# Expert weights loaded as 768 pieces of half a megabyte instead of 384 of one, on a decoder layer with 32 experts

## The reference

```
x = x + W_out( sigmoid(Ga h) * HGRN2(h) + sigmoid(Gb h) * MultiScalePool(h) ),   h = RMSNorm(x)
x = x + MoE_top4of32(RMSNorm(x))
x = x + sigmoid(RMSNorm(x) W_pg) * (p W_pp),   then a final RMSNorm

gate = min(xb @ w_gate[e] + b_gate[e], 7);  up = clip(xb @ w_up[e] + b_up[e], -7, 7)
y    = ((up + 1) * gate * sigmoid(1.702 * gate)) @ w_down[e] + b_down[e]
```

## Time and profile before

| | |
|---|---|
| median of 3 runs | 1330.59 us |
| the profiled execution's own time | 1328.84 us |
| its span | 1326.8 us |
| TensorE busy | 1236.3 us, 93% of the span |
| VectorE, ScalarE, GpSimd busy | 25%, 14%, 5% |
| moved by DMA | 462.48 MB, 349 GB/s over the span |
| mean granted TensorE clock | 0.99 |

### The profile page before, as it was taken

One profiled execution on the slowest core, in us unless ns is written; L12 is line 12 of the kernel. 1 busy time (PEld: TensorE's weight loads), 2 busy tenths in 40 slices (PEclk: granted clock), 3 DMA queues, 4 the chain that ended last, 5 costly groups with the idle time before them and its releaser, 6 DMA issues.

```text
span 1326.8 us, 15719 instructions
## 1 busy us (share of the span) xinstructions
PE 1236.3 (93%) x6207; PEld 563.6 (42%) x6207; DVE 331.1 (25%) x644; ACT 179.1 (14%) x353; POOL 72.5 (5%) x155
## 2 busy tenths in 40 slices
PE   6999998999999999999998989899899989999996
PEld 5755444465443443434333333434333333434332
DVE  2423435043412212122111212112111212212123
ACT  3315213112100101101000101101000101100022
POOL 7021120030000000000000000000000000000001
PEclk9999998998999999999999999999999999999999
DMA  9836372394499999999999999999999999999950
GB/s 331 276 126 237 116 285 65 129 386 175 168 422 420 422 422 422 422 422 422 422 422 422 422 422 422 422 422 421 423 422 422 422 421 423 422 422 420 422 227 34
DMA packets 80531, 462.48 MB, mean 349 GB/s; under 512 B 8681, under 2 KB 9865, under 8 KB 31344
## 3 DMA queue, kind: packets, MB, share of 16 engines
q1 hardware_dynamic: 73968, 444.16, 81.7%
q0 software_dynamic: 3840, 12.85, 3.1%
q10 hardware_dynamic: 2688, 4.98, 1.1%
HBM read 456.04 MB, written 6.39 MB: 349 GB/s over the span
## 4 chain that ended last, share of the span: by engine, by line
PE 70%; DMA 24%; DVE 2%; ACT 1%; issue 1%; SPq 1%; POOLq 0%; POOL 0%; DVEq 0%; ACTq 0%
PE bank L1016 34%; DMA arena<-in_w_down_dram 22%; PE bank L660 10%; PE bank L1073 5%; PE bank L702 3%; PE bank L957 3%; PE bank L1107 2%; PE bank L852 2%; DMA arena<-in_w_up_dram 2%; PE bank L683 1%; PE bank L967 1%; PE bank L1037 1%; PE bank L629 1%; SPq L426 1%; PE bank L984 1%
## 5 line engine op out<-in xcount | busy, mean ns | idle before, releaser
L1016 PE MATMUL bank<-arena 128*64 128x512 f32 x3072 | 678.6, 595 | 46.5 <-DMA arena<-in_w_up_dram 31.3
L1016 PEld LDWEIGHTS bank<-arena 128*64 128x64 f32 x3072 | 228.5, 137 | 481.2 <-issue 481.0
L660 PE MATMUL bank<-arena 128*128 128x512 f32 x320 | 143.3, 605 | 3.8 <-ACT arena L1166 2.9
L660 PEld LDWEIGHTS bank<-arena 128*128 128x128 f32 x320 | 60.7, 193 | 81.2 <-issue 78.0
L1784 DVE TENSOR_TENSOR arena<-bank,arena 128x512 f32<-128x512 f32 (+1 forms) x96 | 61.6, 682 | 75.6 <-PE bank L1073 75.4
L1073 PE MATMUL bank<-arena 128*128 128x512 f32 (+1 forms) x192 | 74.6, 601 | 0.9 <-DVE arena L1777 0.9
L957 PEld LDWEIGHTS bank<-arena 128*128 128x128 f32 x512 | 62.8, 196 | 25.6 <-issue 25.6
L1777 DVE COPY arena<-bank 128x512 f32<-128x512 f32 x16 | 11.1, 691 | 239.2 <-PE bank L1016 239.2
L1766 DVE TENSOR_SCALAR arena<-bank 128x512 f32<-128x512 f32 x32 | 20.6, 685 | 199.9 <-PE bank L1016 199.9
L957 PE MATMUL bank<-arena 128*128 128x128 f32 x512 | 69.1, 288 | 0.0
L1760 DVE TENSOR_SCALAR arena<-bank 128x512 f32<-128x512 f32 x32 | 20.6, 685 | 189.2 <-PE bank L1016 189.2
(11 more groups left out here) (244 smaller groups left out, 731.2 us busy)
## 6 DMA issues: line engine op xcount, KB each, us to landing
arena<-in_w_gate_dram SPq DMA_DIRECT2D x128, 1024.0 KB, 26.4
arena<-in_w_up_dram SPq DMA_DIRECT2D x128, 1024.0 KB, 26.6
arena<-in_w_down_dram SPq DMA_DIRECT2D x128, 1024.0 KB, 26.2
arena<-in_w_in_dram SPq DMA_DIRECT2D x14, 2048.0 KB, 12.3
out_dram<-arena POOLq DMA_DIRECT2D x9, 512.0 KB, 5.7
arena<-in_state_hgrn_dram POOLq DMA_DIRECT2D x8, 512.0 KB, 14.9
arena<-sample_values ACTq DMA_DIRECT2D x8, 512.0 KB, 6.4
arena<-in_w_out_dram SPq DMA_DIRECT2D x4, 1024.0 KB, 8.0
```

The lines of the kernel that those rows point to most:

```text
L660: ins = pe.matmul(job_bank(name)[:, :], hT[:, k, toks(t)], w[:, k, :], start=(k == 0), stop=(k == KD - 1))
L1016: ins = pe.matmul(out[c][hp(one), :], src[:, k * P + CAP * one:k * P + CAP * one + CAP], w[one][:, j, halves(c)], start=(first and k == 0) ...
```

## The change

A granule becomes 128 rows (4 KB for each partition), half a megabyte, and the ring gets 32 places of half the size in the same memory. There are 8 granules a matrix, 48 a pair, 768 in all, and 32 load semaphores. The rows of a granule are now consecutive, so columns of tokens are taken in plain blocks of 128. `products` waits for two granules before each 8 records where it waited before each 16, and releases each after these. The sixteen counts of `s_used` before the experts give 2 each. `w_ple_gate` comes in 8 pieces of half a megabyte with one 4 KB row for each partition.

```diff
-GRAN = 2048
+GRAN = 1024
-RING = 16
+RING = 32
...
-        wout = view(R + 8 * GRAN, 8192).rearrange("p (k n) -> p k n", k=KD)
+        wout = view(R + 16 * GRAN, 8192).rearrange("p (k n) -> p k n", k=KD)
...
-        gran = [view(HG + (g - 8) * GRAN if 8 <= g < 12 else R + (g if g < 8 else g - 4) * GRAN, GRAN).rearrange(
-            "p (j n) -> p j n", j=2) for g in range(RING)]
+        gran = [view(HG + (g - 16) * GRAN if 16 <= g < 24 else R + (g if g < 16 else g - 8) * GRAN, GRAN)
+                for g in range(RING)]
...
-            parts = [w.rearrange("o e (g p j) n -> (o e) g p j n", j=2, p=P) for w in (w_gate, w_up, w_down)]
-            ple = w_ple_gate[0].rearrange("(g j p) n -> g p j n", j=2, p=P)
+            parts = [w.rearrange("o e (g p) n -> (o e) g p n", p=P) for w in (w_gate, w_up, w_down)]
+            ple = w_ple_gate[0].rearrange("(g p) n -> g p n", p=P)
...
-                        for g in range(4):
+                        for g in range(KD):
                             for one in range(2):
-                                at_ = 2 * NGRAN * n + 8 * m + 2 * g + one
+                                at_ = 2 * (NGRAN * n + KD * m + g) + one
                                 sp.wait_ge(s_used, 2 * NGRAN * i + at_ + 1)
                                 sp.dma_start(gran[at_ % RING], parts[m][e + 2 * n + one, g])\
                                   .then_inc(s_gr[at_ % RING], 16)
...
-                for g in range(4):
+                for g in range(KD):
                     sp.wait_ge(s_used, used + g)
                     sp.dma_start(gran[g], ple[g]).then_inc(ld["ple"], 16)
-                sp.wait_ge(s_used, used + 5)
+                sp.wait_ge(s_used, used + 10)
...
-                                ins.then_inc(s_used, 1)
+                                ins.then_inc(s_used, 2)
...
-            def every_other(k):
-                first = 2 * P * (k // 2) + k % 2
-                return slice(first, first + 2 * P - 1, 2)
+            def slice_of(k):
+                return slice(k * P, (k + 1) * P)
...
-                    for g in range(4):
-                        if m == 2 and g % 2 == 0:
-                            pe.wait_ge(s_aTs, 2 * i + g // 2 + 1)
-                        if m == 0 and g == 2:
+                    for k in range(KD):
+                        if m == 2 and k % 4 == 0:
+                            pe.wait_ge(s_aTs, 2 * i + k // 4 + 1)
+                        if m == 0 and k == 4:
                             pe.wait_ge(s_xe, 2 * i + 2)
-                        w = list(granules(m, g))
-                        for j in range(2):
-                            k = 2 * g + j
-                            for c in range(2):
-                                for one in range(2):
-                                    ins = pe.matmul(out[c][hp(one), :],
-                                                    src[:, k * P + CAP * one:k * P + CAP * one + CAP],
-                                                    w[one][:, j, halves(c)], start=(first and k == 0),
-                                                    stop=(k == KD - 1))
-                                    if m == 1 and k == 0 and c == 0 and one == 0:
-                                        ins.then_inc(s_used, 1)
-                                    if j == 1 and c == 1 and not (g == 3 and one == 1):
-                                        ins.then_inc(s_used, 1)
+                        w = list(granules(m, k))
+                        for c in range(2):
+                            for one in range(2):
+                                ins = pe.matmul(out[c][hp(one), :],
+                                                src[:, k * P + CAP * one:k * P + CAP * one + CAP],
+                                                w[one][:, halves(c)], start=(first and k == 0),
+                                                stop=(k == KD - 1))
+                                if m == 1 and k == 0 and c == 0 and one == 0:
+                                    ins.then_inc(s_used, 1)
+                                if c == 1 and not (k == KD - 1 and one == 1):
+                                    ins.then_inc(s_used, 1)
...
-                pe.wait_ge(ld["ple"], 128 if r else 64)
+                pe.wait_ge(ld["ple"], 256 if r else 128)
```

More of the change, by code:

```diff
@@ L807, in _ @@
                 o, cc = job_bank(name), slice(c * P, (c + 1) * P)
-                pe.matmul(o[:, 0:144], u[:, 0, cc], band0[g], start=True, stop=True, skip_group_check=True).then_inc(s_used, 1)
+                pe.matmul(o[:, 0:144], u[:, 0, cc], band0[g], start=True, stop=True, skip_group_check=True).then_inc(s_used, 2)
                 pe.matmul(o[:, P:SEQ], u[:, 1, cc], band1[g], start=False, stop=True, skip_group_check=True)
@@ L838, in weights @@
             def weights(w, k, half):
-                return gran[k // 2][:, k % 2, halves(half)] if w is None else w[:, k, halves(half)]
+                return w[:, k, halves(half)]
             def quarter(w, k, n):
-                return gran[k // 2][:, k % 2, cols(2, n)] if w is None else w[:, k, cols(2, n)]
+                return w[:, k, cols(2, n)]
             def product(tag, t, src, w, slices=KD):
@@ L956, in gather @@
                     for t in range(2):
-                        ins = pe.matmul(XG[k // 4][:, (k % 4) * P:(k % 4 + 1) * P], h2[:, t, every_other(k)], oh[:, t, :],
+                        ins = pe.matmul(XG[k // 4][:, (k % 4) * P:(k % 4 + 1) * P], h2[:, t, slice_of(k)], oh[:, t, :],
                                         start=(k % 4 == 0 and t == 0), stop=False, skip_group_check=True)
@@ L966, in gather_samples @@
                         rows = slice(32 * c, 32 * c + NS)
-                        ins = pe.matmul(XG[c][:, k * P:(k + 1) * P], h2[rows, 2, every_other(4 * c + k)], oh[rows, 2, :],
+                        ins = pe.matmul(XG[c][:, k * P:(k + 1) * P], h2[rows, 2, slice_of(4 * c + k)], oh[rows, 2, :],
                                         start=False, stop=True, skip_group_check=True, tile_position=(32 * c, 0))
@@ L974, in turn_half @@
                     k = 4 * c + j
-                    ins = pe.transpose(out[c][:, j * P:(j + 1) * P], src[:, every_other(k)], ident)
+                    ins = pe.transpose(out[c][:, j * P:(j + 1) * P], src[:, slice_of(k)], ident)
                 return ins
@@ L995, in pair, with granules @@
                 i = i0 + n
-                def granules(m, g):
+                def granules(m, k):
                     for one in range(2):
-                        turn, place = divmod(2 * NGRAN * n + 8 * m + 2 * g + one, RING)
+                        turn, place = divmod(2 * (NGRAN * n + KD * m + k) + one, RING)
                         pe.wait_ge(s_gr[place], i0 * (16 * 2 * NGRAN // RING) + 16 * (turn + 1))
@@ L1004, in products @@
                 def products(m, out, src, first):
-                    for g in range(4):
-                        if m == 2 and g % 2 == 0:
-                            pe.wait_ge(s_aTs, 2 * i + g // 2 + 1)
-                        if m == 0 and g == 2:
+                    for k in range(KD):
+                        if m == 2 and k % 4 == 0:
+                            pe.wait_ge(s_aTs, 2 * i + k // 4 + 1)
+                        if m == 0 and k == 4:
                             pe.wait_ge(s_xe, 2 * i + 2)
-                        w = list(granules(m, g))
-                        for j in range(2):
-                            k = 2 * g + j
-                            for c in range(2):
-                                for one in range(2):
-                                    ins = pe.matmul(out[c][hp(one), :],
-                                                    src[:, k * P + CAP * one:k * P + CAP * one + CAP],
-                                                    w[one][:, j, halves(c)], start=(first and k == 0),
-                                                    stop=(k == KD - 1))
-                                    if m == 1 and k == 0 and c == 0 and one == 0:
-                                        ins.then_inc(s_used, 1)
-                                    if j == 1 and c == 1 and not (g == 3 and one == 1):
-                                        ins.then_inc(s_used, 1)
-                        if last and m == 2 and g == 0:
@@ L1025, in products @@
+                        if last and m == 2 and k == 1:
                             pe.wait_ge(s_c, i + 1)
                             project("", 1, 1)
-                        if last and m == 2 and g == 1:
+                        if last and m == 2 and k == 3:
                             project("", 2, 0)
@@ L1106, in gate @@
                         for n in ((half,) if t < 2 else range(4)):
-                            ins = pe.matmul(piece(("pg" + r, t, n)), xT[:, k, toks(t)], gran[k // 2][:, k % 2, cols(t, n)],
+                            ins = pe.matmul(piece(("pg" + r, t, n)), xT[:, k, toks(t)], gran[k][:, cols(t, n)],
```

## The result

The changed kernel takes 1378.72 us (median of 4 runs, 1377.18 to 1380.22) against 1330.57 of the kernel before beside it: a ratio of 1.0365, 95% interval 1.0347 to 1.0383. The time lies just inside the stated range (1334 to 1380) and on the forecast side, but the forecast was 1357: the rate did what the sum said, and 21 us came from something that the sum had at nothing.

The account below looks back on a forecast made before the run. The prediction took the expert stage to be bound by DMA at 421.9 GB/s. Rows +30.5, start -2.0 and end -1.8 gave +26.7 us, 1355.5 on the profiled execution and 1357 us in the runs' terms, range 1334 to 1380.

Parts of the forecast that it names:

- the sum: Whole kernel: 30.5 - 2.0 - 1.8 = +26.7 us, with the rate at 408 GB/s; 1357 us in the runs' terms.
- What bounds the kernel: Expert stage: DMA-bound from 350.37 us to the last up granule; a round needs 59.7 us of DMA, 54.7 of TensorE.
- Rows of 4 KB, +30.5 us: Expert weight loads: 4 KB packets lower the rate from 421.9 to 408 GB/s over 377.5 * 10^6 bytes, +30.5 us.
- The line between 8 KB and 2 KB: Expert loads: straight line in a megabyte's time, 9.3 ns a row, putting 4 KB rows at 409.6 GB/s; 408 was taken.
- The start, -2.0 us: Start of the expert stage: finer release lets the first waiting load go 8 records earlier, -2.0 us.
- The end, -1.8 us: Last up granules: with half granules, 8 of 16 records are done before the last piece lands, -1.8 us.
- Twice the issues: SyncE's issues in the DMA-bound stretch: 0.40 us needed of 1.285 us a half piece, so costed at nothing.
- A: Rival on expert loads: contiguous 4 KB rows run at 417 GB/s like `w_out`, +6.7 us, 1337 us; chance 0.14.
- B: Rival on expert loads: rate stays 421.9 GB/s and finer release and wait win, 1326.8 us; chance 0.07.
- C: Rival on expert loads: each piece costs 0.06 to 0.075 us too, 397 to 399 GB/s, about 1381 us; chance 0.12.
- The 2.0 us fixed: Each load DMA: the skill's fixed 2.0 us, unhidden over 720 half pieces, would add hundreds of microseconds; given no chance.
- The signs listed: Changed kernel's profile: slices at 408 GB/s, about 245 MB in 600 us, rounds of 61.7 us, landing after some 14 us.

Follow-up runs that it names:

- rows of 16 KB with a step of four: Kernel before with 2 MB granules, 16 KB rows, ring of 8, token columns with a step of four: 1377.99 us, ratio 1.0354.
- one wait for two pieces: Changed kernel, but SyncE waits once for the places of both experts' pieces, then issues the two: 1354.89 us, ratio 1.0175.
- rows of 4 KB alone: Kernel before with 1 MB granules kept, but 4 KB rows and token columns in plain blocks: 1358.69 us, ratio 1.0194.
- two DMAs, even and odd: Kernel before, each 1 MB granule loaded by two DMAs, on even and on odd partitions, 8 KB rows: 1331.91 us, ratio 1.0007.
- long loop body: Kernel before, but SyncE's loop body covers four rounds instead of two, 96 issues: 1340.07 us, ratio 1.0054.
- GpSimd's waits: Kernel before plus 4096 GpSimd instructions that only wait on a count already reached, 32 instruction packets: 1352.16 us, ratio 1.0154.
- changed, straight line: Changed kernel with SyncE's loop written out, 768 issues and no jump back: 1357.66 us, ratio 1.0194.

## Why the prediction was partly right

**What bounds the kernel**: right. Every run whose loads changed their rate moved as a DMA-bound stretch does, but for the rows of 16 KB with a step of four, where TensorE took over.

**Rows of 4 KB, +30.5 us**: right in mechanism and nearly in size. The rate is 409 to 410 and not 408. With one wait for two pieces, from the first released issue (349.95) to the last up wait's end (1276.17) are 926.2 us; before, 350.37 to 1249.01, 898.6: +27.6. The kernel with rows of 4 KB alone has 925.4, +26.8. The line between 8 KB and 2 KB had said 409.6, which gives +26.9; the better estimate was on the page, and I took the other for being in the steady state. The line also held outside its range, at 16 KB (428 expected, 429 measured).

**The start, -2.0 us**: from first product to first released issue 3.6 us (346.76 to 350.35 in the changed kernel) instead of 5.0, so -1.4. It is lost in the start of the stage itself, which came 1.4 us later, so the first released load went out at the same time in both (350.35 and 350.37). The stage started between 345.4 and 349.3 us in these kernels, and the profile of the kernel before is the odd one: its granted clock stays at 1.00 from 60 to 72 us, where in the others it dips to between 0.66 and 0.77 for some 4 us. The other kernels with pieces of 1 MB start at 348.9 to 349.3 and issue 5.2 to 5.4 us later; those with half a megabyte start at 346.3 to 346.8 and issue 3.6 to 3.7 us later. So the finer release is worth 1.7 us; why the latter also start the stage earlier is not explained here.

**The end, -1.8 us**: right. The last waits of the changed kernel:

```profile
1297.08 1.94 PE L1013 MATMUL bank<-arena 128*64 128x512 f32 x8 [0.62 <-DMA arena<-in_w_up_dram]
1299.64 1.94 PE L1013 MATMUL bank<-arena 128*64 128x512 f32 x8 [0.62 <-DMA arena<-in_w_up_dram]
```

From 1299.64 to the end of the span (1375.7) are 76.1 us, against 77.8 before: -1.7.

**"Twice the issues ... I cost the issues at nothing"**: this is the step that failed. I set their time (0.40 us of 1.28) against SyncE's room, and that was right; I did not ask how long the loop body becomes. It grows from 114 to 226 instructions, counted in the compiled program (178 still fit), so it is fetched anew in every turn. What this costs is read best from the DMA-bound stretch alone: from the first released issue to the last products that wait for an up piece, with the instruction packets (queue 14) that came in it.

| kernel | stretch, us | packets | us for each packet |
|---|---|---|---|
| before | 898.6 | 0 | |
| two DMAs, even and odd | 899.2 | 1 | |
| long loop body | 909.1 | 17 | 0.61 |
| GpSimd's waits | 917.7 | 32 | 0.60 |
| rows of 4 KB alone | 925.4 | 0 | |
| changed, one wait for two | 926.2 | 1 | |
| changed, straight line | 928.1 | 6 | 0.4 |
| changed | 949.3 | 36 | 0.66 |

(The price is against the kernel before, for the straight line and the changed kernel against one wait for two.) So the changed kernel's 48.9 us on the span (1375.7 against 1326.8) are, within 0.1, 27.6 for the rows, 23.1 for the packets, -1.7 at the end and nothing at the start. Its rounds are 63.2 us apart (752.93 to 1005.72 in four of its chain of waits), 1.7 more than 25.17 MB need at 409.6, and five packets in two rounds are 3.3. The growing dips fit too: 12 packets had come before the third jump, so the one engine was some 8 us behind (an estimate, 12 times 0.66). Of the 15.6 us of pieces under way a stop of 5.7 leaves 9.9, and when the lag comes near that the fifteen run dry at the jump. From the fourth jump on each dip costs 3.4 us (369 in place of 410 over 34.4 us), which is what five packets cost. With 26.9 us under way and a lag of at most 10.4, the long body never comes near it.

The Trainium skill ("Runtime: NRT & Kernel Launch", Instruction fetch mechanics) has the rule that bore on this: a taken branch whose target is no longer held forces a fetch that the engine waits for. The trace agrees (5.7 us without an issue at the jump), but the runs put the cost elsewhere, in the time of one DMA engine. The section calls fetching in a straight line mostly hidden; for the data stream it was not, since GpSimd's 4096 instructions cost it 19 us, and the measurement decides.

**The rivals.** A is out by the rows of 4 KB alone, B by every rate. C came out nearest in time and is wrong in its mechanism: its price for each piece was worked out from differences of 0.03 us, and even and odd halves show that a piece costs nothing (0.6 us for 384 more). Its upper price is also mis-worked: 2.645 us a megabyte is 396.4 GB/s and +57.5 us, not 397 and +56, which changes nothing here. It was this rival that brought the range to 1380; the time fell inside by 1.3 us, for a reason that I had not named, and that is luck. The 2.0 us fixed that the prediction set aside is given in the Trainium skill ("DMA: Bandwidth & Descriptors", Anatomy of one DMA) for DMAs that GpSimd issues; SyncE's pieces here are no test of it.

**The signs listed.** Landing after 15.6 us (14 expected), issues of 0.95 us (0.9), the group waits of 0.62 us: right. Three were off: 239.6 MB in 600 us instead of 245, rounds of 63.2 us instead of 61.7, and slices of 369, below the 403 that I had named as a sign of a wrong forecast. They were the signs of the fault.

Open: why a packet whose like takes 0.31 us (8 KB at 1/16 of 422 GB/s) costs its engine twice that, and why a turn needs five packets. In the trace each issue of line 426 is a MOVE and a DMA_DIRECT2D (159 of each for `w_gate` from 600 to 1200 us), so the body of 226 has 322 instructions that way (the one that fits, 274). GpSimd's packets held 128 instructions each; 322 fill two and a half.

## What to carry to other kernels

When a DMA-bound loop issues more, smaller pieces, the number of pieces is free (half a megabyte against one, with the queue full) but the bytes in a row are not (387, 409, 422 and 429 GB/s for rows of 2, 4, 8 and 16 KB), and the loop body must not grow so long that it is fetched anew in every turn, as the one of 226 instructions was and the one of 178 was not. Look at the instruction queue in the DMA view: packets that come back in every turn fall on one of the 16 engines, and a tail at one sixteenth of the rate when the loads end shows that it is behind. Before a layout is made coarser for DMA, move its column step out of TensorE's weight loads.

## What the runs showed of the hardware that I had not expected

- An instruction packet of 8 KB costs a saturated stream 0.60 to 0.66 us, for SyncE's instructions and for GpSimd's, and even if that engine's work has nothing to do with the stream.
- DMAs on 64 neighbouring partitions ran at 221 GB/s (in the profiled execution), on every other partition at 422, with all 16 engines busy in both (shares 1.02 and 1.01). This agrees with the Trainium skill ("SBUF — State Buffer", Door 1: The DMA port swizzle), by which partitions 0 to 63 reach only 8 of 16 ports.
- Float32 weight loads of 128x128 take 191 to 196 ns with a column step of one or two and 328 ns with four.
- Pieces under way, as the time from issue to landing: 26.9 us of 1 MB with 8 KB rows, 18.4 us of 1 MB with 4 KB rows, 15.6 us of half a megabyte with 4 KB rows; the queue holds neither a number of bytes nor of pieces alone.
